# Entry of the up projections in another order, and the sums of the gated branches on GpSimd in three of four up pairs

## The reference

```python
h = x @ w_in + b_in            # 1024 x 1024 by 1024 x 5376: q, k, v and gates of two mixers, two merge gates
o_a = swa_sink_attention(rope(q_a), rope(k_a), v_a, sinks) * silu(gate_a)
o_b = stick_breaking_attention(q_b, k_b, v_b) * silu(gate_b)
merged = sigmoid(mg_a) * (o_a @ w_up_a) + sigmoid(mg_b) * (o_b @ w_up_b)   # the up projections
out = layer_norm(ALPHA * x + merged @ w_out)
```

## Time and profile before

| what | value |
| --- | --- |
| median of 3 runs | 724.59 us (724.15 to 725.71) |
| span of the profiled execution | 723.8 us, 0.8 us under the median; the page gives no other time for it |
| TensorE busy | 709.9 us, 98% |
| VectorE busy | 561.4 us, 78% |
| ScalarE busy | 447.3 us, 62% |
| GpSimd busy | 103.2 us, 14% |

### The profile page before, as it was taken

One profiled execution on the slowest core, in us unless ns is written; L12 is line 12 of the kernel. 1 busy time (PEld: TensorE's weight loads), 2 busy tenths in 40 slices (PEclk: granted clock), 3 DMA queues, 4 the chain that ended last, 5 costly groups with the idle time before them and its releaser, 6 DMA issues.

```text
span 723.8 us, 10890 instructions
## 1 busy us (share of the span) xinstructions
PE 709.9 (98%) x3998; PEld 579.6 (80%) x3998; DVE 561.4 (78%) x782; ACT 447.3 (62%) x776; POOL 103.2 (14%) x130
## 2 busy tenths in 40 slices
PE   8999999999999999999999999999998999899996
PEld 7788877777888888788878888888887888788885
DVE  6999788766987987998888774577779999790644
ACT  7954477676766767686687754655587555560421
POOL 0000000000322332232222210000000000000782
PEclk9999999999999999999999999999999999999998
DMA  8235332231110101010012214674333554460451
GB/s 300 108 93 126 103 103 74 73 102 44 44 36 24 60 30 59 15 73 31 30 48 99 73 56 141 225 266 162 110 117 132 167 168 159 146 239 24 159 187 60
DMA packets 44404, 77.27 MB, mean 107 GB/s; under 512 B 12352, under 2 KB 16960, under 8 KB 44352
## 3 DMA queue, kind: packets, MB, share of 16 engines
q1 hardware_dynamic: 44352, 76.59, 31.6%
HBM read 55.60 MB, written 18.87 MB: 103 GB/s over the span
## 4 chain that ended last, share of the span: by engine, by line
PE 93%; DVE 2%; DMA 2%; issue 1%; ACT 1%; SPq 1%; POOL 0%; DVEq 0%; ACTq 0%; POOLq 0%
PE ps L230 26%; PE ps L232 25%; PE ps L231 25%; PE ps L1822 5%; PE ps L1834 5%; PE ps L1807 4%; DMA raw<-in_w 2%; PE ps L1751 1%; PE ps L1763 1%; PE ps L1732 1%; DVE keep L1482 1%; PE ps L1786 0%; ACT w_hi L798 0%; PE ps L1720 0%; SPq L665 0%
## 5 line engine op out<-in xcount | busy, mean ns | idle before, releaser
L230 PE MATMUL ps<-x_hi,w_hi 128*128 128x512 f32 x416 | 167.4, 402 | 0.6 <-DVE x_lo L1389 0.6
L232 PE MATMUL ps<-x_hi,w_lo 128*128 128x512 f32 x416 | 162.5, 391 | 0.0
L231 PE MATMUL ps<-x_lo,w_hi 128*128 128x512 f32 x416 | 162.2, 390 | 0.0
L1281 DVE TENSOR_TENSOR w_lo<-raw,w_hi 128x512 fp32r<-128x512 f32 x144 | 97.8, 694 | 48.0 <-ACT w_hi L798 47.5
L230 PE MATMUL ps<-t_ops,w_hi 128*128 128x512 f32 x288 | 116.0, 403 | 2.3 <-issue 2.3
L232 PE MATMUL ps<-t_ops,w_lo 128*128 128x512 f32 x288 | 112.9, 392 | 0.0
L231 PE MATMUL ps<-t_ops,w_hi 128*128 128x512 f32 x288 | 112.9, 392 | 0.0
L1482 DVE TENSOR_TENSOR_SCAN keep<-keep 128x895 f32<-128x895 f32 (+4 forms) x64 | 86.2, 1376 | 15.3 <-POOL keep L750 15.3
L230 PEld LDWEIGHTS ps<-x_hi,w_hi 128*128 128x128 f32 x416 | 78.3, 188 | 16.7 <-issue 2.3
L232 PEld LDWEIGHTS ps<-x_hi,w_lo 128*128 128x128 f32 x416 | 78.1, 188 | 16.9
L231 PEld LDWEIGHTS ps<-x_lo,w_hi 128*128 128x128 f32 x416 | 78.4, 188 | 14.6
(11 more groups left out here) (212 smaller groups left out, 1186.8 us busy)
## 6 DMA issues: line engine op xcount, KB each, us to landing
raw<-in_w SPq DMA_DIRECT2D x28, 512.0 KB, 3.8
raw<-in_w SPq DMA_DIRECT2D x50, 256.0 KB, 2.6
sig_m<-sig_d SPq DMA_DIRECT2D x16, 512.0 KB, 4.7
sig_d<-sig_m SPq DMA_DIRECT2D x28, 256.0 KB, 2.5
xr<-in_xt SPq DMA_DIRECT2D x16, 256.0 KB, 5.9
o_t<-o_d SPq DMA_DIRECT2D x8, 512.0 KB, 4.9
raw<-in_xn SPq DMA_DIRECT2D x8, 512.0 KB, 3.6
out<-o_t SPq DMA_DIRECT2D x16, 256.0 KB, 2.2
```

Of the source, the lines that this page charges most:

```text
L230: pe.matmul(out, w_hi, x_hi, start=first, stop=False, skip_group_check=goes_on)
L231: pe.matmul(out, w_hi, x_lo, start=False, stop=False, skip_group_check=goes_on)
L232: return pe.matmul(out, w_lo, x_hi, start=False, stop=last, skip_group_check=goes_on)
L1281: dve.tensor_tensor(ring_slot(w_lo, q), part_of(q), ring_slot(w_hi, q).bitcast(F32), ALU.subtract).then_inc(part_lo, 1)
```

## The change

The fourth sum of quarters (position 6's operand) moves from VectorE to GpSimd, and so do the sums of the two gated branches in `merge` for up pairs 0 to 2; pair 3 keeps them on VectorE, on a semaphore of its own (`m_last`). The tables of the entry are written out for each branch: ScalarE rounds the operand of position 4 after product 138 rather than 139, and those of positions 5 and 6 are spread; on VectorE the last `add_block` of pair 19 comes between the two branches of position 3.

```diff
-UP_SUMS = {122: 1, 125: 2, 128: 3, LAST_PAIR + 2: 4}
-UP_SPLITS = {LAST_PAIR: 0, LAST_PAIR + 1: 1, LAST_PAIR + 3: 2, LAST_PAIR + 4: 3, LAST_PAIR + 6: 4, LAST_PAIR + 7: 5,
-             LAST_PAIR + 9: 6}
+UP_SUMS = {122: 1, 125: 2, 128: 3}
+UP_HIGH = {LAST_PAIR: ((0, 0), (0, 1)), LAST_PAIR + 1: ((1, 0), (1, 1)), LAST_PAIR + 3: ((2, 0), (2, 1)),
+           LAST_PAIR + 4: ((3, 0), (3, 1)), LAST_PAIR + 5: ((4, 0), (4, 1)), LAST_PAIR + 6: ((5, 0),),
+           LAST_PAIR + 8: ((5, 1),), LAST_PAIR + 9: ((6, 0),), LAST_PAIR + 10: ((6, 1),)}
+UP_LOW = {LAST_PAIR: ((0, 0), (0, 1)), LAST_PAIR + 1: ((1, 0), (1, 1)), LAST_PAIR + 3: ((2, 0), (2, 1)),
+          LAST_PAIR + 4: ((3, 0), (3, 1)), LAST_PAIR + 6: ((4, 0), (4, 1)), LAST_PAIR + 7: ((5, 0),),
+          LAST_PAIR + 8: ((5, 1),), LAST_PAIR + 9: ((6, 0),), LAST_PAIR + 10: ((6, 1),)}
...
 SyncE, load_w
                 elif k < 4:
-                    sp.wait_ge(m_set, 4 * (UP_PAIRS - 1) + k - 1)
+                    sp.wait_ge(m_last, k - 1)
...
 GpSimd
+            def fourth_sum(ab):
+                o = up_sum(4, ab)
+                pool.wait_ge(u_raw[2], ab + 1)
+                pool.wait_ge(ol_done, 2 + ab + 1)
+                pool.tensor_tensor(o, o, up_sum(2, ab), ALU.subtract).then_inc(u_raw[4], 1)
+
+            def branches_sum(j, b):
+                m, nh = UP_BLOCKS[b]
+                o = up_made(b)
+                pool.wait_ge(up_mul, 4 * j + b + 1)
+                pool.wait_ge(ol_done, 2 * NP)
+                pool.tensor_tensor(o_t[:, 2 * j + m, half(nh)], o[:, 0, :], o[:, 1, :], ALU.add).then_inc(m_set, 1)
+
+            for ab in range(2):
+                fourth_sum(ab)
+            for j in range(UP_PAIRS - 1):
+                for b in range(4):
+                    branches_sum(j, b)
...
 VectorE, merge
-                dve.wait_ge(up_mul, e + 1)
-                dve.wait_ge(ol_done, 10 if j == 0 else 2 * NP)
-                dve.tensor_tensor(o_t[:, 2 * j + m, half(nh)], o[:, 0, :], o[:, 1, :], ALU.add).then_inc(m_set, 1)
+                if j == UP_PAIRS - 1:
+                    dve.wait_ge(up_mul, e + 1)
+                    dve.tensor_tensor(o_t[:, 2 * j + m, half(nh)], o[:, 0, :], o[:, 1, :], ALU.add).then_inc(m_last, 1)
...
 VectorE, after
-                for ab in range(2):
-                    if q in UP_SPLITS:
-                        branch_lo(UP_SPLITS[q], ab)
-                    if q in UP_SUMS:
+                for pos, ab in UP_LOW.get(q, ()):
+                    branch_lo(pos, ab)
+                    if (pos, ab) == (3, 0):
+                        add_block(N_PAIRS - 1, 2)
+                if q in UP_SUMS:
+                    for ab in range(2):
                         up_sums(UP_SUMS[q], ab)
```

More of the change, by code:

```diff
@@ L500, in build @@
         u_raw = {t: sem(f"u_raw{t}") for t in range(1, 5)}
-        up_mul, m_set = sem("up_mul"), sem("m_set")
+        up_mul, m_set, m_last = sem("up_mul"), sem("m_set"), sem("m_last")
         mh_done, ml_done, wo_hi, wo_lo = sem("mh_done"), sem("ml_done"), sem("wo_hi"), sem("wo_lo")
@@ L707, in _ @@
                 load_w(k)
-            sp.wait_ge(m_set, 4 * UP_PAIRS)
+            sp.wait_ge(m_last, 4)
             sp.dma_start(g_bc, ln_g).then_inc(ln_in, 16)
@@ L993, in split_next @@
                     gate_a_sigmoid(GATE_A_AT.index(q))
-                if q in UP_SPLITS:
-                    for ab in range(2):
-                        branch_hi(UP_SPLITS[q], ab)
+                for pos, ab in UP_HIGH.get(q, ()):
+                    branch_hi(pos, ab)
             for h in range(2):
@@ L1159, in merged_hi @@
             def merged_hi(k):
-                act.wait_ge(m_set, 2 * k + 2 if k < 6 else 4 * UP_PAIRS)
+                if k < 6:
+                    act.wait_ge(m_set, 2 * k + 2)
+                else:
+                    act.wait_ge(m_last, 4)
                 act.wait_ge(product_done, ALL_PRODUCTS - 2 + min(k // 2, 2))
@@ L1315, in up_sums @@
                     dve.tensor_tensor(o, quarter_of(1, 1), up_sum(1, ab), ALU.subtract).then_inc(u_raw[t], 1)
-                elif t == 3:
+                else:
                     dve.wait_ge(u_raw[1], ab + 1)
                     dve.tensor_tensor(o, quarter_of(1, 1), o, ALU.subtract).then_inc(u_raw[t], 1)
[L1319 to L1322, removed]
             def branch_lo(pos, ab):
@@ L1375, in sums @@
                 for k in {1: (0,), 4: (1,), 5: (2,)}.get(pos, ()):
-                    add_block(i, k)
+                    if (i, k) != (N_PAIRS - 1, 2):
+                        add_block(i, k)
                 if pos in (4, 5) and i + 1 < ALL_PAIRS:
```

## The result

The changed kernel takes 729.46 us (median of 6 runs, 727.93 to 729.78), the one before 724.43 beside it (723.94 to 725.71). The ratio is 1.006, 95% interval 1.0049 to 1.0071: slower, by 5.0 us between the medians. The forecast was 725.7, in a range up to 727.7. The span of the profiled execution is 728.1, against 723.8 before: 4.3 apart. In the runs that have both figures, an execution takes 1.7 more than its span (729.78 for the span of 728.1). So the profiled execution of the kernel before took about 725.5, some 1.0 over its median, and that of the changed kernel was 0.3 over its own; this is why the profiles are 0.7 closer than the medians. The 0.8 that the forecast adds to a span of 724.9 isn't the step from span to time, but its difference to the kernel before, 1.1, doesn't hang on it.

What follows compares the result with a forecast made beforehand. TensorE, busy 98% of the span, was taken as the bound, so only its waits or clock could give time back. Span 723.8 + 0.4 entry + 0.7 exit = 724.9, median 0.8 above: 725.7, range 721.0 to 727.7.

Steps and rivals of the forecast that it cites:

- The 0.8: Whole program: the median was put 0.8 above the profiled span, taking the forecast span of 724.9 to 725.7.
- Price of a sum: Anywhere VectorE runs beside GpSimd: a GpSimd sum costs VectorE 1.05 us for 512 elements and 2.15 for 1024.
- Entry, +0.4: Stage entry: TensorE stops 2.6 in product 140, clock falls as before, old wait before 142 goes; 0.4 us slower.
- rival 3: Entry: the clock doesn't fall at the new wait, so the entry gains 0.6 and time is 724.0; chance 0.10.
- Up pairs, nothing: Up pairs: sums cost VectorE 3.7 us more, its waits for ScalarE hide most; TensorE shows nothing until the exit.
- so they take turns: VectorE beside GpSimd: the two alternate, VectorE giving about 0.10 to a mask; basis for pricing sums at 1.05 and 2.15.
- have over 5 us: GpSimd's new sums: nothing queues behind them, and their readers, ScalarE's next copy into the same tile, have over 5 us.
- Exit, +0.7: Output projection's entry: VectorE's waits used up, `merge(2, 3)` and its load 0.7 later, the 2.01 wait grows by 0.7.
- Clock at the exit: Output projection's entry: no term for a changed clock; only the wait of 2.01 grows, by 0.7.
- Rival 2: Whole kernel: VectorE becomes the bound, a sum holding it 1.29; TensorE waits in pairs 21 to 23; 727.7, upper 729.7; chance 0.17.
- Rival 1: Whole kernel: GpSimd doesn't hold VectorE up, VectorE is 2.28 early at the entry; 3.6 faster, 721.0; chance 0.15.

Runs made afterwards that it cites:

- Experiment 4: Changed kernel with GpSimd's 14 sums replaced by zero fills of the same outputs behind the same waits, output not the reference's: 720.61 us, ratio 0.995.
- experiment 2: Changed kernel with the branch sums of all pairs back on VectorE, GpSimd keeping only the two fourth sums: 724.66 us, ratio 1.0006.
- experiment 5: Changed kernel plus a one-column VectorE fill without inputs behind the two low parts, ahead of `v_t`'s multiply, three in all: 726.87 us, ratio 1.0035.
- experiment 6: Changed kernel with the `raw_d` branch sum back on VectorE in pairs 0 to 2, the other sums staying on GpSimd: 726.47 us, ratio 1.0023.
- experiment 9: Changed kernel, but GpSimd asks for `raw_d`'s sum only after VectorE has done `v_t`'s multiply: 728.89 us, ratio 1.0063.
- experiment 10: Changed kernel with `v_t`'s multiply placed ahead of the two low parts in pairs 21 to 23: 729.02 us, ratio 1.0064.
- experiment 1: Changed kernel with both kinds of sums back on VectorE and only the new order of the entry kept: 721.0 us, ratio 0.9954.
- experiment 3: Changed kernel with the two fourth sums back on VectorE, GpSimd keeping the branch sums of pairs 0 to 2: 727.31 us, ratio 1.0036.

## Why the prediction was wrong

The forecast for the profiled execution was +1.1, and it came to +4.3 (between the medians, +5.0).

- **Price of a sum.** It was right where a sum runs beside a busy VectorE: 1.05 and 2.15 forecast, 1.09 and 2.2 measured. Experiment 4 shows that it is the reading that costs. But the forecast charges all 11 sums of the pairs, and in each pair of the changed kernel only those of `raw_c` and `o_b` cost VectorE anything; those of `raw_d` and `v_t` ran while it was idle.
- **Entry, +0.4.** The mechanism was right, its times to about 0.2: first sigmoid forecast for 545.8, started at 546.01; stop 2.6, measured 2.60; read of product 139 done at 548.95, measured 549.11. The clock was rival 3's in the changed kernel's profile (entry -0.96) and the forecast's in that of experiment 2 (+0.36).
- **Up pairs, nothing.** This is the step that failed: "so they take turns", with readers that "have over 5 us". VectorE's price was hidden as forecast: without the lockout TensorE doesn't stop in the pairs (experiments 5 and 6). But a sum that asks can be passed over at each change of VectorE's instructions. `raw_d`'s missed four and took 5.14 instead of 2.3. And the reader had less time than 5 us. That figure fits only from the start of the multiply (570.65); from its end (571.87) ScalarE's read before (576.30) is 4.4 away. After, with TensorE 0.96 early and VectorE late by its turns, the read would have been due near 575.3, some 2.3 behind the ask at 573.00. A sum of 2.3 just fits, one of 5.14 doesn't: 1.37 + 0.49 + 0.51 of stops and three times 0.26, +3.1. How much it is depends on how early TensorE comes. In experiments 9 and 10 the clock fell at the entry, TensorE left it 0.58 and 0.49 late, and the first stop was 0.27 and 0.28 instead of 1.37; product 167 began at 625.00 and 624.91, against 624.53. So most of what the upper clock gave at the entry was lost again in the first stop.
- **Exit, +0.7.** Stop 3.01 instead of 2.7, +1.0 from product 167 to the output projection. The multiply of `merge(2, 3)` started 4.52 ahead of product 167 instead of 5.77, 1.25 less, and the load took 5.23 instead of 5.49. The reason was another than forecast: VectorE had not used up its waits for ScalarE, it had one of 2.82 just before that multiply, behind the locked-out sum. Without the lockout the forecast's reason holds: in experiment 6 VectorE has no wait for ScalarE left in the pairs, and the multiply is 1.06 later.
- **Clock at the exit.** It isn't in the sum: the forecast left it as it was, and in this profile it stayed low for longer, +1.1. It isn't shown to belong to the change: behind stops of 2.99, 2.89 and 2.81 in experiments 5, 6 and 9 the clock stayed at 1.00, 1.6 less than before, and behind one of 2.84 in experiment 10 it was 0.66.

Together, -0.96 + 3.1 + 1.0 + 1.1 = +4.3, with rounding. Rival 2's place (TensorE waits in pairs 21 to 23) was right and its reason was not: VectorE was not the bound there, it idled for 2.81 behind each lockout. That its upper figure, 729.7, lies next to the 729.46 measured is luck. Rival 1, at 721.0, is what experiments 1 and 4 measured (721.0 and 720.6): the value of the new order without the price. That VectorE is relieved of the sums, which is rival 1's reason, adds little to it: product 143 is 3.50 early in experiment 4 and 3.12 in experiment 1, where VectorE still does all sums.

**What stays open.** Why GpSimd is passed over. It repeats: the same sum, all three pairs, with 5.14 to 5.15 in experiments 3 and 10 as well. It ends at VectorE's idle time or at an instruction that reads nothing (5). Other sums of the same kernel, asking beside instructions of the same kinds, are let in at the first change, now and then at the second (2 and 6), and 72 trials outside the kernel show none. At one and the same place `raw_d`'s sum is passed over and `v_t`'s is let in (9 against 6); what in the kernel makes that difference, the tile or how long VectorE's next instruction had been ready, was not found.

## What to carry to other kernels

Work that goes from VectorE to GpSimd isn't free when both read SBUF: here each sum of 512 that VectorE had to wait for cost it 1.1 us where it had taken 0.6, so move only what VectorE has idle time for, or what only writes. Read the deadline of its result from the end of the instruction that releases it to its next reader, and price the transfer with GpSimd coming last, behind the whole stretch in which VectorE has no gap, not with the next turn. And take a change apart before judging it: its order of the entry gained 3.6 us, its GpSimd half lost 8.5, and together they looked like one bad idea.

## What the runs showed of the hardware

- GpSimd's wait for its turn behind VectorE isn't bounded by one instruction: 5.14 us for a sum of 1.28, which waited out five VectorE instructions. The Trainium skill ("SBUF — State Buffer", Who interferes with whom) lets whoever issues first hold the ports for its instruction while the other blocks. The trace agrees for the single pairings (2.31 instead of 1.22) and not for the waiting sum, which had asked before four of the instructions that passed it began.
- A stop of TensorE didn't always bring the lower clock. After the stop of 2.6 near 549 the granted clock was 1.00 in the changed kernel and 0.65 in experiment 2; after stops before the output projection it was 0.66 after 1.90 (experiment 1) and 1.00 after 1.89 (experiment 2). So the length of the stop alone doesn't tell. Two windows, experiment 1 and then experiment 2:

```profile
624.01:628.50 4.49, 4.49 (x13) 3.54 (x14) 4.49 (x4) 4.11 (x5) 0.00 (x0) 0.66 0.00 0
```

```profile
627.48:632.00 4.52, 4.52 (x20) 3.75 (x21) 4.49 (x4) 4.11 (x5) 0.00 (x0) 1.00 0.00 0
```

  The lower clock costs 1.4 to 1.7 us a stop (24 matmuls behind it took 7.20 in experiment 1 and 5.57 in experiment 2), so two stops can move an execution by about 3. Experiment 6 ran from 723.86, with a granted clock of 0.997 over the whole execution, to 728.08, with 0.990; what else is in that spread isn't shown.
